# The second token mixer of a two-block layer, in another order: scores before turns, head norms over the full width, the narrow product behind a value unit

## What is computed

```python
def token_mixer(h, w_in, b_f, lam_q1, lam_k1, lam_q2, lam_k2, subln_g, rel_bias, lambda_init):
    proj = h @ w_in                     # dq, dk, dv, fq, fk, fv: 512 columns each, f_logit: 8
    ...
    cum = jnp.cumsum(jax.nn.log_sigmoid(f_logit), axis=1)
    ...
        sd = jnp.einsum('bqhd,bkhd->bhqk', qd, dk).astype(jnp.float32) * (DIFF_HEAD_DIM ** -0.5)
        sd = sd.reshape(B, DIFF_HEADS, 2, Q_BLOCK, S) + bias[:, None]
        pd = jax.nn.softmax(jnp.where(causal, sd, NEG_2), axis=-1)
        ad = pd[:, :, 0] - lam * pd[:, :, 1]
        od = jnp.einsum('bhqk,bkhe->bqhe', ad.astype(dv.dtype), dv)
        od = rmsnorm(od, subln_g) * (1.0 - lambda_init)
        sf = jnp.einsum('bqhd,bkhd->bhqk', qf, fk).astype(jnp.float32) * (FOX_HEAD_DIM ** -0.5)
        sf = sf + jnp.transpose(cq, (0, 2, 1))[..., :, None] - cum_k[..., None, :]
        pf = jax.nn.softmax(jnp.where(causal, sf, NEG_2), axis=-1)
        of = jnp.einsum('bhqk,bkhd->bqhd', pf.astype(fv.dtype), fv)
```

## Time and profile before

| | |
|---|---|
| median of 3 runs | 891.24 us (890.67 to 892.95) |
| the profiled execution | 890.31 us, span 888.5 us |
| TensorE matmul busy | 857.8 us, 97% |
| VectorE busy | 594.0 us, 67% |
| ScalarE busy | 459.5 us, 52% |
| DMA | 143.82 MB, 162 GB/s over the span |
| the second mixer, from the row scale to the output product | 580.7 to 675.1 us |

### The profile page before, as it was taken

How to read it: one execution, slowest core, us unless ns; L and a number is a source line. 1 busy time by engine, 2 the same in 40 slices (tenths; PEclk the granted TensorE clock), 3 DMA queues, 4 the chain that set the end, 5 groups by cost and what they waited for, 6 DMA issues and landing times.

```text
span 888.5 us, 15550 instructions
## 1 busy us (share of the span) xinstructions
PE 857.8 (97%) x6234; PEld 797.4 (90%) x6234; DVE 594.0 (67%) x780; ACT 459.5 (52%) x649; POOL 60.5 (7%) x64
## 2 busy tenths in 40 slices
PE   7999799999999999999999999999999999999997
PEld 6999799999888998899999999888987899999995
DVE  5548875536776677688777677776664685555554
ACT  5457744328665444476555554655565443333332
POOL 0026700000000142000000000000000000000000
PEclk9999899999999999999999999999999999999999
DMA  8634353233433345645455455343324355555531
GB/s 346 248 111 143 113 195 120 95 107 121 168 118 141 121 169 173 228 166 195 174 190 194 183 190 190 143 163 138 131 91 151 134 189 214 186 184 185 186 135 47
DMA packets 22167, 143.82 MB, mean 162 GB/s; under 512 B 2928, under 2 KB 3188, under 8 KB 5728
## 3 DMA queue, kind: packets, MB, share of 16 engines
q1 hardware_dynamic: 20304, 138.30, 43.6%
q0 software_dynamic: 1808, 4.73, 1.6%
HBM read 141.96 MB, written 1.84 MB: 162 GB/s over the span
## 4 chain that ended last, share of the span: by engine, by line
PE 83%; DVE 6%; ACT 5%; issue 3%; POOL 2%; DMA 1%; SPq 0%; POOLq 0%; ACTq 0%; DVEq 0%
PE pj L467 17%; PE pj L470 14%; PE pj L469 14%; PE pa L892 6%; PE pa L893 6%; PE pa L894 6%; PE pj L471 2%; PE pj L472 2%; PE pa L506 2%; DVE w_lo L1614 2%; ACT w_hi L1155 1%; PE pj L570 1%; PE pj L576 1%; PE pj L572 1%; POOL area L415 1%
## 5 line engine op out<-in xcount | busy, mean ns | idle before, releaser
L1614 DVE TENSOR_TENSOR w_lo<-w_raw,w_hi 128x2048 fp32r<-128x2048 f32 x127 | 294.4, 2320 | 75.7 <-ACT w_hi L1155 75.7
L467 PE MATMUL pj<-a_hi,w_hi 128*128 128x256 f32 x1168 | 334.4, 286 | 0.6 <-issue 0.6
L469 PE MATMUL pj<-a_lo,w_hi 128*128 128x256 f32 x1168 | 331.6, 284 | 0.0
L470 PE MATMUL pj<-a_hi,w_lo 128*128 128x256 f32 x1168 | 331.5, 284 | 0.0
L1155 ACT ACTIVATE w_hi<-w_raw 128x2048 fp32r<-128x2048 f32 x127 | 242.0, 1907 | 57.2 <-PE pa L894 41.7
L467 PEld LDWEIGHTS pj<-a_hi,w_hi 128*128 128x128 f32 x1168 | 225.1, 193 | 5.6 <-issue 4.6
L469 PEld LDWEIGHTS pj<-a_lo,w_hi 128*128 128x128 f32 x1168 | 225.2, 193 | 0.8
L470 PEld LDWEIGHTS pj<-a_hi,w_lo 128*128 128x128 f32 x1168 | 225.2, 193 | 0.0
L892 PE MATMUL pa<-w_hi,a_hi 128*128 128x512 f32 x280 | 109.4, 391 | 2.6 <-issue 2.6
L893 PE MATMUL pa<-w_lo,a_hi 128*128 128x512 f32 x280 | 109.2, 390 | 0.0
L894 PE MATMUL pa<-w_hi,a_lo 128*128 128x512 f32 x280 | 108.9, 389 | 0.0
(11 more groups left out here) (272 smaller groups left out, 1031.8 us busy)
## 6 DMA issues: line engine op xcount, KB each, us to landing
w_raw<-stream SPq DMA_DIRECT2D x127, 1024.0 KB, 4.8
area<-gains POOLq DMA_DIRECT2D x4, 512.0 KB, 4.4
cst<-consts SPq DMA_DIRECT2D x1, 1093.0 KB, 12.9
x_tok<-x_in SPq DMA_DIRECT2D x2, 512.0 KB, 4.1
w_raw<-stream SPq DMA_DIRECT2D x4, 256.0 KB, 6.2
area<-cmpw POOLq DMA_DIRECT2D x1, 1024.0 KB, 5.4
out<-x_tok SPq DMA_DIRECT2D x4, 256.0 KB, 2.0
t_wide<-t_rows POOLq DMA_DIRECT2D x1, 768.0 KB, 10.8
```

The lines of the kernel that those rows point to most:

```text
L467: pe.matmul(out_, a[0], a[1], start=first, stop=False)
L469: pe.matmul(out_, wh, al, start=False, stop=False)
L470: return pe.matmul(out_, wl, ah, start=False, stop=last)
L1614: dve.tensor_tensor(w_lo[:, slot, :], w_raw[:, slot, :], w_hi[:, slot, :].bitcast(F32), ALU.subtract)\
```

## The change

TensorE's list in the second mixer gets another order: the scores of the next round stand in front of the turn of the round (d1 to d3, f0 to f2), and for that the splits, copies and exponentials on the other two engines are reordered. Unit dv0 now runs first, then d0's scores, then the narrow product, whose turn comes behind dq1. The head norms: the squares are added with two products of 128x512 whose stationary operand is all ones, so that each partition holds the sum for every token, in the banks of fq1 and fk1; ScalarE takes the root of all 1024 numbers a partition, VectorE their reciprocal in one instruction and then one product with `od`. The eight one-column products, the diagonal and the two products on it are gone. f3's scores use the common region. PSUM banks are declared one by one.

```diff
-        pj3 = pb("pj", [P, 3, 512])
-        pj = [pj3[:, i, :] for i in range(3)]
+        pj = [pb(f"pj{i}", [P, 512]) for i in range(3)]
...
-        od, odsq, dg8, odn = V(50, 4, T), V(0, 4, T), V(4, 8, P), V(0, 4, T)
+        od, odsq, od_root, odn = V(50, 4, T), V(0, 4, T), V(4, 4, T), V(0, 4, T)
...
-        f3_first, f3_last = [b for b in range(3) if b != BANK[("fv", 1)][0]]
-        ps3 = pj3[:, f3_first:f3_last + 1:f3_last - f3_first, :]
+        od_banks = (BANK[("fq", 1)][0], BANK[("fk", 1)][0])
 
         def fo(j):
 
-            return pj[f3_first][:, 0:T] if j % 2 else po[:, 0:T]
+            return pj[BANK[("fk", 1)][0]][:, 0:T] if j % 2 else po[:, 0:T]
 
...
-            claim(pe, "O", "flog")
-            pe.wait_ge(S("ws_ready"), 2)
-            narrow_products(8)
...
             def f_scores(j):
-                if j < 3:
-                    claim(pe, "S", f"f{j}")
-                else:
-                    await_value(pe, ("fk", 1))
-                    await_value(pe, ("fv", 0))
+                claim(pe, "S", f"f{j}")
...
-                if j == 1:
-                    pe.wait_ge(S("f3_read"), 1)
...
+            run_unit(("dv", 0))
             d_scores(0)
-            run_unit(("dv", 0))
+            claim(pe, "O", "flog")
+            pe.wait_ge(S("ws_ready"), 2)
+            narrow_products(8)
+            run_unit(("dq", 1))
             narrow_turn("flog_tok", 8)
-            run_unit(("dq", 1))
+            d_scores(1)
             d_turn(0)
-            d_scores(1)
             run_unit(("dk", 1))
             d_apply(0)
+            d_scores(2)
             d_turn(1)
             run_unit(("dv", 1))
             d_apply(1)
-            d_scores(2)
+            d_scores(3)
             run_unit(("fq", 0))
             f_sums()
             d_turn(2)
-            d_scores(3)
             run_unit(("fk", 0))
             d_apply(2)
             d_turn(3)
+            f_scores(0)
             run_unit(("fq", 1))
             d_apply(3)
-            f_scores(0)
+            f_scores(1)
             run_unit(("fk", 1))
             f_turn(0)
-            f_scores(1)
-
-            claim(pe, "O", "odn")
+
+            await_value(pe, ("fq", 1))
+            await_value(pe, ("fk", 1))
             pe.wait_ge(S("od_sq_ready"), 1)
-            for h in range(4):
-                for tb in range(2):
-                    mm = pe.matmul(po[:, 2 * h + tb:2 * h + tb + 1], odsq[:, h, tb * P:(tb + 1) * P], ones[:, 0:1],
-                                   start=True, stop=True)
-            written(mm, "O")
+            for q in range(2):
+                mm = pe.matmul(pj[od_banks[q]][:, :], ones, odsq[:, 2 * q:2 * q + 2, :], start=True, stop=True)
+            mm.then_inc(S("od_sums"), 1)
+            f_scores(2)
             run_unit(("fv", 0))
             f_turn(1)
-            f_scores(2)
             f_scores(3)
             f_apply(0)
+            pe.wait_ge(S("od_root"), 2)
             run_unit(("fv", 1))
             f_turn(2)
             f_apply(1)
-
-            claim(pe, "S", "odn")
-            pe.wait_ge(S("dg8_ready"), 1)
-            for q in range(2):
-                mm = pe.matmul(ps[:, q, :], ones, dg8[:, 4 * q:4 * q + 4, :], start=True, stop=True)
-            written(mm, "S")
             f_turn(3)
             f_apply(2)
             f_apply(3)
             pe.wait_ge(S("odn_hi"), 1)
             pe.wait_ge(S("odn_lo"), 1)
-            await_read(pe, "S", "odn")
+            await_read(pe, "S", "f3")
...
             ahead(("dv", 0))
+            token_major(("dv", 0), dv[:, :, 0:256])
...
             exps(8, sm2, pr2)
-            token_major(("dv", 0), dv[:, :, 0:256])
+            ahead(("dq", 1))
             await_psum(act, "O", "flog_tok")
             read(act.activation(fl, po[:, 0:128].rearrange("p (b x) -> p b x", b=2)[:, :, 0:8], ACT.Copy), "O")
-            ahead(("dq", 1))
             act.wait_ge(S("flx_ready"), 1)
             A.did(act.activation(lf_e, fl, ACT.Abs))
             A.sync()
...
+            act.activation(lf_e, lf_e, ACT.Ln, bias=1.0).then_inc(S("lfe_ready"), 1)
             d_turned(0)
-            act.activation(lf_e, lf_e, ACT.Ln, bias=1.0).then_inc(S("lfe_ready"), 1)
+            exps(9, sm2, pr2)
             ahead(("dk", 1))
-            exps(9, sm2, pr2)
+            ahead(("dv", 1))
             d_turned(1)
+            exps(10, sm2, pr2)
             token_major(("dv", 1), dv[:, :, 256:512])
             d_out(0)
             ahead(("fq", 0))
-            exps(10, sm2, pr2)
+            exps(11, sm2, pr2)
             await_psum(act, "O", "fcum")
             read(act.activation(ncum, po[:, 0:T], ACT.Copy, scale=-1.0), "O")
             d_turned(2)
             ahead(("fk", 0))
-            exps(11, sm2, pr2)
             d_turned(3)
             ahead(("fq", 1))
+            exps(12, sm2, pr2)
             d_out(1)
             await_read(act, "O", "d1")
             act.activation(odsq, od, ACT.Square).then_inc(S("od_sq_ready"), 1)
             ahead(("fk", 1))
-            exps(12, sm2, pr2)
+            exps(13, sm2, pr2)
+            ahead(("fv", 0))
             f_turned(0)
-            await_psum(act, "O", "odn")
+            act.wait_ge(S("od_sums"), 1)
             act.wait_ge(S("lm_ready"), 1)
-            read(act.activation(ods, po[:, 0:8], ACT.Sqrt, bias=lm[:, 2:3], scale=1.0 / 128), "O")
-            exps(13, sm2, pr2)
+            for q in range(2):
+                act.activation(od_root[:, 2 * q:2 * q + 2, :], pj[od_banks[q]][:, :].rearrange("p (a t) -> p a t", a=2), ACT.Sqrt, bias=lm[:, 2:3],
+                               scale=1.0 / 128).then_inc(S("od_root"), 1)
+            exps(14, sm2, pr2)
+            act.wait_ge(S("odn_ready"), 1)
+            act.activation(a_hi[:, 8:12, :], odn, ACT.Copy, scale=1.0 - LAMBDA_INIT).then_inc(S("odn_hi"), 1)
             token_major(("fv", 0), fv[:, :, 0:256])
             f_turned(1)
+            f_out_hi(0)
             ahead(("fv", 1))
-            exps(14, sm2, pr2)
-            f_out_hi(0)
             exps(15, sm2, pr2)
+            token_major(("fv", 1), fv[:, :, 256:512])
             f_turned(2)
-            token_major(("fv", 1), fv[:, :, 256:512])
             f_out_hi(1)
             f_turned(3)
-            act.wait_ge(S("odn_ready"), 1)
-            await_read(act, "S", "odn")
-            act.activation(a_hi[:, 8:12, :], odn, ACT.Copy, scale=1.0 - LAMBDA_INIT).then_inc(S("odn_hi"), 1)
             f_out_hi(2)
             f_out_hi(3)
...
-            narrow_out("flog", 8)
...
+            ahead(("dv", 0))
             d_soft(0)
-            ahead(("dv", 0))
+            narrow_out("flog", 8)
             d_probs(0)
+            ahead(("dq", 1))
+            channel_major(("dq", 1), dq[:, 2:4, :], 64.0 ** -0.5)
             await_read(dve, "O", "flog_tok")
             tt(fl, fl, prm_("b_f").unsqueeze(1).to_broadcast([P, 2, 8]), ALU.add).then_inc(S("flx_ready"), 1)
-            ahead(("dq", 1))
-            channel_major(("dq", 1), dq[:, 2:4, :], 64.0 ** -0.5)
             d_soft(1)
             dve.wait_ge(S("lfe_ready"), 1)
             for tb in range(2):
...
                     lf_e[:, tb].unsqueeze(1).to_broadcast([P, 16, 8]), ALU.min, ALU.subtract)\
                     .then_inc(S("lf_ready"), 1)
             ahead(("dk", 1))
+            channel_major(("dk", 1), dk[:, 2:4, :])
             d_probs(1)
-            channel_major(("dk", 1), dk[:, 2:4, :])
+            d_soft(2)
             ahead(("dv", 1))
-            d_soft(2)
+            d_probs(2)
+            d_soft(3)
             ahead(("fq", 0))
-            d_probs(2)
             channel_major(("fq", 0), fq[:, 0:2, :], 64.0 ** -0.5)
-            d_soft(3)
+            d_probs(3)
             ahead(("fk", 0))
-            d_probs(3)
             channel_major(("fk", 0), fk[:, 0:2, :])
+            f_soft(0)
             ahead(("fq", 1))
+            f_probs(0)
             channel_major(("fq", 1), fq[:, 2:4, :], 64.0 ** -0.5)
-            f_soft(0)
+            f_soft(1)
             ahead(("fk", 1))
-            f_probs(0)
             channel_major(("fk", 1), fk[:, 2:4, :])
-            f_soft(1)
-
-            await_read(dve, "O", "odn")
-            V_.did(dve.reciprocal(ods, ods))
+            f_probs(1)
+            f_soft(2)
+            dve.wait_ge(S("od_root"), 2)
+            V_.did(dve.reciprocal(od_root, od_root))
             V_.sync()
-            tt(dg8, ident.unsqueeze(1).to_broadcast([P, 8, P]), ods.unsqueeze(2).to_broadcast([P, 8, P]), ALU.mult)\
-                .then_inc(S("dg8_ready"), 1)
-            f_probs(1)
+            stt(odn, od, prm_("subln"), od_root, ALU.mult, ALU.mult).then_inc(S("odn_ready"), 1)
             ahead(("fv", 0))
-            f_soft(2)
+            f_probs(2)
             f_soft(3)
-            f_out_lo(0)
-            f_probs(2)
-            ahead(("fv", 1))
-            f_probs(3)
-            f_out_lo(1)
-
-            await_psum(dve, "S", "odn")
```

(14 more changed lines are left out.)

41 lines of the change are left out of this document (16 added, 25 removed).

## The result

The changed kernel takes 894.58 us (median of 11 runs, 892.77 to 897.15), the kernel before, run beside it, 890.70 (11 runs, 888.71 to 892.95). The ratio is 1.0042, with a 95% interval of 1.003 to 1.0054: slower by 3.7 us, between 2.7 and 4.8. The forecast was 893.9, 2.7 us more than before, so it held, at the lower end of what was measured.

What follows compares the result with a forecast made beforehand. TensorE, busy for 97% of the span, was taken to bound the kernel. Differences of its timeline summed to +0.8 us, plus 1.9 for the clock: 891.24 + 0.8 + 1.9 = 893.9, range 890.6 to 896.4.

Steps and rivals of the forecast that it cites:

- part 1: Unit dv0 in front of the narrow product, which waited for VectorE's rbc copy: a gain of 0.35 us.
- part 2: Turn of d1: scores(d2) waits 3.4 us for VectorE's dk1 copy, the turn 0.8 more; a loss of 2.65.
- part 3: Head norms: one-column matmuls go (1.81 us) and unit fv0 loses its slow clock (1.47); a gain of 3.3.
- part 4: Norm formed before f2's probabilities, so the hole in front of the output product goes: a gain of 1.43 us.
- part 5: Reciprocal on all 1024 numbers on VectorE takes 6.5 us, so apply(f0) waits: a loss of 3.1.
- part 6: Granted clock falls behind the two new TensorE holes: a loss of 1.9 us, bounds 0 and 3.
- The two mechanisms: New TensorE holes: 3.4 us at scores(d2) behind VectorE's dk1 copy, 3.1 at apply(f0) behind the reciprocal.
- (b): Rival: VectorE's reciprocal runs at 8 passes or more, lengthening apply(f0)'s wait; 896.0 us, chance 0.12.
- (c): Rival: reciprocal streams at a plain pass's pace, no hole at apply(f0), at most one clock fall; 889.7 us, chance 0.08.
- rival (a): The two TensorE holes come without a fall of the clock: 892.0 us, chance 0.12.

Runs made afterwards that it cites:

- fill_holes: Changed kernel with six unread 128x256 matmuls on TensorE in each of its two holes; ratio 1.0015 to the kernel before.
- thin_back: Changed kernel with the 16 one-column matmuls put back, unread, in front of the two products with ones; ratio 1.0079 to the kernel before.
- recip_half: Changed kernel with the norm's reciprocal taken of 512 of the 1024 elements a partition; ratio 0.9992 to the kernel before.
- ln_exp: Changed kernel with 1/root formed as exp(-0.5 ln) on ScalarE, without VectorE's reciprocal; ratio 0.9995 to the kernel before.
- recip_16: Changed kernel with the norm's reciprocal taken of 16 of the 1024 elements a partition; ratio 0.999 to the kernel before.
- norm_high_late: Changed kernel with ScalarE's high half of the norm moved behind the fv0 copy and turned f1, reciprocal kept; ratio 1.0013 to the kernel before.
- high_half_first: Changed kernel with fq0's high half ahead of the exponentials of d1 on ScalarE; ratio 1.0005 to the kernel before.
- ln_exp_exps_first: Changed kernel with exp(-0.5 ln) for the reciprocal, d1's probabilities and dk1's copy early on VectorE, forget gate's Ln behind d1's exponentials; 883.72 us, ratio 0.9924.
- wide_for_thin: Kernel before with the 16 one-column matmuls replaced by five wide ones of about the same time; ratio 0.9993 to the kernel before.
- copy_first: Changed kernel with VectorE's copy of dk1 and probabilities of d1 ahead of fq0's low half; ratio 1.0018 to the kernel before.

## Where the prediction was right and wrong

| term of the sum | predicted | in the trace of after |
|---|---|---|
| part 1, dv0 in front of the narrow product | -0.35 | -0.3 (1.06 behind the spread, not 1.35) |
| part 2, hole at scores(d2) | 3.4 | 3.30 |
| part 2, wait at the turn of d1 | 0.8 | 0.72 at full clock (fill_holes), covered in after |
| part 3, thin matmuls | -1.81 | gone; 1.78 long when put back (thin_back) |
| part 3, clock in fv0 | -1.47 | -1.47 (5.85, from 655.20 to 661.05), by two edits |
| part 4, hole at the output product | -1.43 | -1.4, and a new wait of 0.17 at f3's turn |
| part 5, the reciprocal | 6.5 | 6.54 |
| part 5, hole at apply(f0) | 3.1 | 3.10 |
| the sum without the clock behind the holes | +0.8 | +1.1 (fill_holes, 95.60 - 94.46) |
| part 6, clock behind the holes | +1.9 | +2.2 (fill_holes); over 1 us more where a fall is long |

- **The two mechanisms were right**, and each fell away when its cause did. The total didn't come from errors that cancel: no part is off by more than 0.3. Parts 1 and 4 have no run of their own and are read from the rows of after alone. In part 5 the terms add up to 3.2 and not to the 3.1 written; VectorE's maxima took 2.04 and not 2.1 (655.20 to 657.24). What decided part 2 was to read both queues around the moved scores, and not TensorE's order alone. What decided part 5 was the slope of two small reciprocals, carried from 16 elements to 1024, which recip_half and the row of after bear out. Rivals (b) and (c) fall with the one row of 6.54 us, rival (a) with the rows at 0.50. By the section "First, the fixed hardware budget" of "VectorE: DVE Perf Modes" in the Trainium skill, which gives a repeat count of 8, my estimate was 9 us; the row has 6.54, and the measurement decides: 6.25 ns an element is 5.6 times the low half's 1.12 (2.29 us for 2048).
- **Part 6 was sized too small for some executions.** I priced each fall at under one unit's loss. In the profile of after both falls last about 3.4 us. In ln_exp the same hole of 3.3 was followed by this:

```profile
607.00:608.00 1.00, 0.00 (x0) 0.99 0.00 0
608.00:609.00 1.00, 0.56 (x4) 0.50 0.38 49
...
614.00:615.00 1.00, 1.00 (x7) 0.60 0.00 0
```

  and dv1 took 7.67, not 6.28. Of the six profiled executions in which hole one stands empty (after, recip_16, recip_half, thin_back, norm_high_late, ln_exp), the last two show the long fall, the other four have dv1 at 6.3 to 6.4. A long fall is worth 1.3 us. Each run also lists the mean granted clock of every execution, and in after the time goes with it: the three at 0.985 and 0.986 took 895.2 to 897.2 us, the four at 0.990 took 892.8 to 894.1. Part of that lies outside the stage, in code that no kernel here changes: near 209 us a fall of 3.4 us stands in most profiles, none in high_half_first, recip_half, fill_holes and ln_exp_exps_first, and one of 6.8 in norm_high_late. So that after came out at +3.7 and not +2.7 can be such falls, in the stage or in front of it; which of them it was is not shown, and the interval holds 2.7 as well.
- **Part 3 named half of its cause.** The sentence that thin matmuls are to blame and the 1.47 comes back holds for after; wide_for_thin shows that in the old order it would not have come back, since the clock fell behind the scores instead. I had looked for thin matmuls and idle time, and not at the 64-row and 8-row scores standing back to back.
- **What stays open:** why the fall lasts 3.4 us in one execution and nearly 7 in another of the same code; and the gaps between stage and medians, 1.7 us in copy_first and 1.3 in ln_exp_exps_first.

## What to carry to other kernels

When matmuls are moved ahead, follow what their operands' copies are queued behind on the other engines: here a copy of 0.7 us stood behind a conversion of 2.3 that waited 4.7 and was wanted only by unit fq0, 10 us on. A reciprocal that was cheap on 8 numbers a partition (0.20 us) isn't on 1024; fit its slope from the small rows first, and form 1/root as exp(-0.5 ln) where the activation engine has the time. A wait of 3 us on TensorE cost here about a third more than its length through the clock (2.2 us on 6.4), and that part varies between executions.
